# A decoder step whose decode work is moved ahead of stick-breaking and takes six of the sixteen gate chunks, with half of each expert's down projection split

## The reference

```python
u = rmsnorm(x, g_mix); z = u @ w_in        # 1024 -> 3*768 + 3*512 + 2*1024 columns
qa, ka, va, qb, kb, vb, ga, gb = split(z)
oa = combine_groups([dilated(qa[g], ka[g], va[g]) for g in 3 groups])   # 3 x 4 heads
ob = stick_breaking(qb, kb, vb)                                         # 8 heads
x = x + (sigmoid(ga) * (oa @ w_oa) + sigmoid(gb) * (ob @ w_ob)) @ w_out
x = x + hier_moe(rmsnorm(x, g_moe))        # 32 experts, top 2: (silu(v@w_gate) * (v@w_up)) @ w_down
y = rmsnorm(x + sigmoid(rmsnorm(x, g_ple) @ w_pg) * (p @ w_pp), g_final)
```

## Time and profile before

| | us |
|---|---|
| median of 3 runs | 2231.35 (2228.87 to 2236.27) |
| the profiled execution | 2228.89 |
| its span | 2227.3 |
| PE busy in it | 1855.4 (83%) |
| DVE busy | 1057.1 (47%) |
| ACT busy | 800.7 (36%) |
| mean granted clock of TensorE | 0.911 |

### The profile page before, as it was taken

One profiled execution on the slowest core, in us unless ns is written; L12 is line 12 of the kernel. 1 busy time (PEld: TensorE's weight loads), 2 busy tenths in 40 slices (PEclk: granted clock), 3 DMA queues, 4 the chain that ended last, 5 costly groups with the idle time before them and its releaser, 6 DMA issues. The chain is left out here.

```text
span 2227.3 us, 26881 instructions
## 1 busy us (share of the span) xinstructions
PE 1855.4 (83%) x9852; PEld 1443.3 (65%) x9852; DVE 1057.1 (47%) x1415; ACT 800.7 (36%) x1096; POOL 128.4 (6%) x181
## 2 busy tenths in 40 slices
PE   5999999789999947632498992599999999996698
PEld 4999999777777835431295541466666677773585
DVE  5211211158888733335151224466666666662674
ACT  4111111147666503220040000454555555452454
POOL 0111111100000000010031003000000000001110
PEclk7999999989999978675699995699999999998799
DMA  3443444245221160025354213899999999994620
GB/s 114 116 121 114 131 126 122 92 140 172 67 86 39 39 180 1 1 55 152 99 167 145 76 39 137 354 390 379 381 384 385 382 385 382 382 378 164 224 75 39
DMA packets 165325, 401.73 MB, mean 180 GB/s; under 512 B 25659, under 2 KB 102955, under 8 KB 144772
## 3 DMA queue, kind: packets, MB, share of 16 engines
q1 hardware_dynamic: 146004, 334.32, 41.8%
q0 software_dynamic: 10320, 33.82, 5.3%
q10 hardware_dynamic: 8928, 32.63, 3.6%
HBM read 325.80 MB, written 82.61 MB: 183 GB/s over the span
## 5 line engine op out<-in xcount | busy, mean ns | idle before, releaser
L87 PE MATMUL p_acc<-uh,p_wl 128*128 128x344 f32 x720 | 234.9, 326 | 13.0 <-DVE ul L293 9.0
L89 PE MATMUL p_acc<-uh,p_wh 128*128 128x344 f32 x720 | 230.6, 320 | 0.0
L88 PE MATMUL p_acc<-ul,p_wh 128*128 128x344 f32 x720 | 230.5, 320 | 0.0
L1891 PE MATMUL x_Y<-x_wd,x_hT 128*128 128x512 f32 x512 | 225.1, 593 | 0.8 <-DVE x_hT L1989 0.8
L305 DVE COPY p_zk<-p_tp 128x512 f32<-128x512 f32 (+1 forms) x90 | 44.2, 547 | 304.4 <-PE p_tp L226 304.4
L1973 DVE TENSOR_TENSOR x_wgl<-x_wg,x_wgh 128x2048 fp32r<-128x2048 f32 x64 | 143.9, 2290 | 49.8 <-ACT x_wgh L1930 49.8
L1891 PEld LDWEIGHTS x_Y<-x_wd,x_hT 128*128 128x128 f32 x512 | 95.0, 190 | 108.2 <-issue 107.1
L269 ACT ACTIVATE p_zc<-p_acc 128x344 f32<-128x344 f32 x90 | 41.2, 458 | 321.6 <-PE p_acc L89 321.6
L1973 DVE TENSOR_TENSOR x_wul<-x_wu,x_wuh 128x2048 fp32r<-128x2048 f32 x64 | 143.8, 2289 | 17.8 <-ACT x_wuh L1930 17.8
L87 PEld LDWEIGHTS p_acc<-uh,p_wl 128*128 128x128 f32 x720 | 135.8, 189 | 18.0 <-issue 14.9
L545 PE MATMUL g_acc<-uh,g_wl 128*128 128x344 f32 x384 | 129.1, 336 | 9.3 <-ACT u L576 7.1
(11 more groups left out here) (316 smaller groups left out, 3676.8 us busy)
## 6 DMA issues: line engine op xcount, KB each, us to landing
x_wg<-in_w_gate SPq DMA_DIRECT2D x64, 1024.0 KB, 7.7
x_wu<-in_w_up SPq DMA_DIRECT2D x64, 1024.0 KB, 7.4
x_wd<-in_w_down SPq DMA_DIRECT2D x32, 2048.0 KB, 12.5
x_x<-xs SPq DMA_DIRECT2D x32, 512.0 KB, 11.6
ys<-x_y ACTq DMA_DIRECT2D x32, 512.0 KB, 11.8
zT<-p_zc ACTq DMA_DIRECT2D x30, 516.0 KB, 3.4
p_w<-in_w_in SPq DMA_DIRECT2D x30, 512.0 KB, 5.5
ztok<-p_zk POOLq DMA_DIRECT2D x30, 512.0 KB, 4.6
```

The lines of the kernel that those rows point to most:

```text
L87: pe.matmul(out, w_low, m_high, start=first, stop=False)
L88: pe.matmul(out, w_high, m_low, start=False, stop=False)
L89: return pe.matmul(out, w_high, m_high, start=False, stop=last)
L1891: last = pe.matmul(Y[c][:, :], hT[:, k, :], wd[:, b, k, c * 512:(c + 1) * 512], start=(k == 0), stop=(k == KF - 1))
```

## The change

Three edits come together. `decode` becomes `decode_and_gates` and is called ahead of `stick_and_gates`; it takes the first six chunks of gates, and `stick_and_gates` the other ten. In it the attention outputs are computed feature-major at once: the value rows are the stationary operand and the weights of all heads the moving one, so that a product for every pair of heads and features comes out, of which DVE keeps the right ones by a mask and a sum (`own_heads`). The key pages have a buffer of their own (`e_pk`), so that their loads need not wait for K and Q. In `experts`, two of the four k-tiles of `w_down` and of the hidden rows are cut into high and low parts, and `down` uses `products` for them.

```diff
+DECODE_GATES = 6
...
-def stick_and_gates(nc, g):
+def stick_and_gates(nc, g, c0):
...
-        CH = 2 * KD
+        CH = 2 * KD - c0
...
             def load_gate(c):
                 need(sp, gwl_full, c)
-                sp.dma_start(gw[:, :, :], win_v[:, :, QKV + c * P:QKV + (c + 1) * P]).then_inc(gw_in, 16)
+                sp.dma_start(gw[:, :, :], win_v[:, :, QKV + (c0 + c) * P:QKV + (c0 + c + 1) * P]).then_inc(gw_in, 16)
...
-def decode(nc, g):
-
-
...
+def decode_and_gates(nc, g, chunks):
...
-        D_SCORES_T, D_PROBS_T, D_VALUES, D_OUT_T = 3, 4, 5, 7
-        S_SCORES_T, S_WEIGHTS_T, S_VALUES, S_OUT_T = 9, 11, 12, 15
...
+        M = KD * 3
+        GROUPS = chunks * NSPLIT
+        D_SCORES_T, D_PROBS_T, D_VALUES = 6, 7, 8
+        S_SCORES_T, S_WEIGHTS_T, S_VALUES = 13, 14, 16
+        STEPS = GROUPS + 2
+        S_SCORES = {9: (0, 1), 10: (1, 3), 11: (3, 5), 12: (5, 8)}
+        cut_at = {max(0, (c - 1) * NSPLIT): c for c in range(1, chunks)}
...
+            cached(sp, K, 0, 0, kq_in)
+            query(0)
+            sp.wait_ge(cleared, 2)
+            for x in (1, 2):
+                cached(sp, K, 0, x, kq_in)
+                query(x)
+            for x in range(N_DIL):
+                own_row(sp, K, A_W, x, kq_in)
+                own_row(sp, Q, 0, x, kq_in)
...
+            sp.wait_ge(table_in, 16)
+            for b in range(2):
+                for x in range(PG):
+                    load_page(PK, b, x, 0, ek_in[b])
+            cached(sp, V, 1, 0, v_in)
+            sp.wait_ge(cleared, 3)
+            for x in (1, 2):
+                cached(sp, V, 1, x, v_in)
+            for x in range(N_DIL):
+                own_row(sp, V, 2 * A_W, x, v_in)
+            for b in range(2, DEC):
+                for x in range(PG):
+                    load_page(PK, b, x, 0, ek_in[b])
+            sp.wait_ge(scored, 2)
             for b in range(DEC):
-                sp.dma_start(e_bias[b * H_B:(b + 1) * H_B, :], g["b_sb"].rearrange("a (h x) -> (a h) x", x=1))\
-                    .then_inc(ebias_in, 16)
-            sp.wait_ge(table_in, 16)
-            for c in range(CH):
-                if c == D_SCORES_T - 1:
-                    sp.wait_ge(scored, 2)
-                    load_pages(0, ek_in)
-                if c == S_SCORES_T:
-                    sp.wait_ge(es_full, DEC * PG)
-                    load_pages(1, ev_in)
+                for x in range(PG):
+                    load_page(PV, b, x, 1, ev_in)
+            for j in range(2):
+                sp.wait_ge(g_out[j], 16 * ((chunks + 1 - j) // 2))
...
+            def own_heads(dst, src, full, heads):
+                dve.wait_ge(full, 1)
+                n = src.shape[1]
+                m = masked[:, 0:n * DEC * heads].rearrange("p (c b h) -> p c b h", c=n, b=DEC)
+                for c in range(n):
+                    ins = dve.tensor_tensor(m[:, c, :, :], src[:, c, :, :],
+                                            own[:, c, 0:heads].unsqueeze(1).to_broadcast([P, DEC, heads]), ALU.mult)
+                    if c < n - 1:
+                        ins.then_inc(dve_step, 1)
+                        steps[0] += 1
+                    else:
+                        then(ins)
+                dve.tensor_reduce(dst, m, AX, ALU.add).then_inc(done, 1)
+
...
+            cut(0)
+            for n in range(STEPS):
+                if n in cut_at:
+                    cut(cut_at[n])
+                if n == D_SCORES_T - 4:
+                    dilated_scores(0)
+                    dilated_scores(1)
+                if n == D_SCORES_T:
...
+                for b in range(*S_SCORES.get(n, (0, 0))):
+                    stick_scores(b)
...
+            def cut(c):
+                act.wait_ge(gw_in, 16 * (c + 1))
+                need(act, acc_full, (c - 1) * NSPLIT)
+                act.activation(gwh[:, c % 2, :, :], gw[:, :, :], ACT.Copy).then_inc(gwh_full, 1)
+                if c + 1 < chunks:
+                    act.wait_ge(gwl_full, c + 1)
+                    load_gate(c + 1)
...
+            def gates(grp):
+                c, x = divmod(grp, NSPLIT)
+                t = slice(x * NS, (x + 1) * NS)
+                pe.wait_ge(gwl_full, c + 1)
+                need(pe, gate_full, grp - 2)
+                for kk in range(KD):
+                    last = products(pe, acc[grp % 3][:, 0:NS], gwh[:, c % 2, kk, :], gwl[:, c % 2, kk, :], uh[:, kk, t],
+                                    ul[:, kk, t], kk == 0, kk == KD - 1)
+                last.then_inc(acc_full, 1)
...
+            def outputs_T(o, rows_, weights, heads, b0, b1):
+
+                for b in range(b0, b1):
+                    for c in range(o.shape[1]):
+                        for x in range(2):
+                            last = pe.matmul(o[:, c, b, :], rows_(x, b)[:, c * P:(c + 1) * P],
+                                             weights[:, x, b * heads:(b + 1) * heads], start=(x == 0), stop=(x == 1),
+                                             skip_group_check=True)
+                return last
...
+                    outputs_T(oT_ps, lambda x, b: V[:, x, b, :], pT, H_G, 0, DEC).then_inc(oT_full, 1)
...
+                if n in (S_VALUES, S_VALUES + 1):
+                    if n == S_VALUES:
+                        pe.wait_ge(aT_read, 1)
+                        pe.wait_ge(ev_in, 16 * DEC * PG)
+                    b0 = (n - S_VALUES) * DEC // 2
+                    last = outputs_T(eoT_ps, lambda x, b: PV[:, b, x, :], aT, H_B, b0, b0 + DEC // 2)
+                    if n > S_VALUES:
+                        last.then_inc(eoT_full, 1)
+                if n < GROUPS:
+                    gates(n)
...
+        KS = KF // 2
+        wdh, wdl = (sb(n, [P, KS, D], F32R) for n in ("wdh", "wdl"))
+        hh, hl = (sb(n, [P, KS, P], F32R) for n in ("hh", "hl"))
+        hT = sb("hT", [P, KF - KS, P])
...
-                pe.wait_ge(hT_full, n + 1)
+                pe.wait_ge(hl_full, n + 1)
                 pe.wait_ge(d_in[b], it * 16 + 16)
                 need(pe, y_read, n * 2)
                 for k in range(KF):
+                    if k < KS:
+                        pe.wait_ge(dl_full, n * KS + (k + 1))
                     for c in range(2):
-                        last = pe.matmul(Y[c][:, :], hT[:, k, :], wd[:, b, k, c * 512:(c + 1) * 512],
-                                         start=(k == 0), stop=(k == KF - 1))
+                        cols = slice(c * 512, (c + 1) * 512)
+                        if k < KS:
+                            last = products(pe, Y[c][:, :], hh[:, k, :], hl[:, k, :], wdh[:, k, cols], wdl[:, k, cols],
+                                            k == 0, False)
+                        else:
+                            last = pe.matmul(Y[c][:, :], hT[:, k - KS, :], wd[:, b, k, cols], start=False,
+                                             stop=(k == KF - 1))
                 last.then_inc(d_used, 1)
...
+            def high_down(n, b, it):
+                act.wait_ge(d_in[b], it * 16 + 16)
+                need(act, d_used, n)
+                for k in range(KS):
+                    act.activation(wdh[:, k, :], wd[:, b, k, :], ACT.Copy).then_inc(dh_full, 1)
+
+            def high_hidden(n):
+                act.wait_ge(tph_full, n + 1)
+                act.activation(hh[:, :, :], tph[:, 0:KS, :], ACT.Copy).then_inc(hh_full, 1)
...
             def step(it, j):
-                one, three = lag(it, j, 1), lag(it, j, 3)
+                one, two, three = lag(it, j, 1), lag(it, j, 2), lag(it, j, 3)
                 new = it * 2 + j
                 if three:
                     output(*three)
+                if two:
+                    high_down(*two)
                 if one:
                     sigmoid(one[0])
+                if two:
+                    high_hidden(two[0])
                 high(new, wg, wgh, wg_in, g_full, gh_full)
...
                 output(last - 1, 0, np_ - 1)
+                high_down(last, 1, np_ - 1)
+                high_hidden(last)
                 output(last, 1, np_ - 1)
...
-                dve.tensor_copy(hT[:, :, :], tph[:, :, :]).then_inc(hT_full, 1)
+                dve.wait_ge(hh_full, n + 1)
+                dve.tensor_copy(hT[:, :, :], tph[:, KS:KF, :]).then_inc(hT_full, 1)
+                dve.tensor_tensor(hl[:, :, :], tph[:, 0:KS, :], hh[:, :, :], ALU.subtract).then_inc(hl_full, 1)
+
+            def low_down(n, b):
+                for k in range(KS):
+                    dve.wait_ge(dh_full, n * KS + (k + 1))
+                    dve.tensor_tensor(wdl[:, k, :], wd[:, b, k, :], wdh[:, k, :], ALU.subtract).then_inc(dl_full, 1)
...
+                if two:
+                    low_down(two[0], two[1])
...
-            stick_and_gates(nc, g)
+            decode_and_gates(nc, g, DECODE_GATES)
+            stick_and_gates(nc, g, DECODE_GATES)
...
             dilated(nc, g)
-            decode(nc, g)
             clear(nc, range(second, nc.free_semaphores[0]))
```

(6 more changed lines are left out.)

279 lines of the change are left out of this document (119 added, 160 removed).

## The result

| | before | after |
|---|---|---|
| median, us | 2230.11 (4 runs, 2223.57 to 2236.27) | 2203.03 (4 runs, 2197.95 to 2208.75) |
| the profiled execution, its span | 2228.89, 2227.3 | 2207.64, 2206.0 |
| mean granted clock of TensorE | 0.911 | 0.910 |

The ratio is 0.988, 95% interval 0.9837 to 0.9923: faster by 1.2%. The forecast was 2190, with a range of 2164 to 2215: the time came 13 us above it and inside the range, and the gain is 27 us where 41 were forecast.

What follows compares the result with a forecast made beforehand. PE was taken as the bound in stick-breaking (92%, DVE close) and the experts (DMA engines 3% behind). Terms -124 + 134 - 41 - 10 = -41 from 2228.89 gave 2188, 2190 on the median's scale; range 2164 to 2215.

Steps and rivals of the forecast that it cites:

- The case that the forecast described: Whole kernel: the forecast itself, 2190 us with its own range 2177 to 2202, chance 0.50.
- the rival "stretched": New block: one raw gate-weight buffer and late loads make it 156 us, total 2212; chance 0.14.
- Old block -124: Old decode block between `dilated` and `merge`: all its 124 us go.
- New block +134: Decode and six gate chunks ahead of stick-breaking: adds 134 us, bounds 120 to 156.
- K, Q and the gate weights, up to the probabilities at 48: New block's start: loads, cuts and softmax done by 48 us; PE, finished at 41.5, stands 6.5.
- DVE's key products, done at 89.5: New block: two cuts and eight key products of 2.46 us, from 68.5 to 89.5; PE stands 8 us.
- the last part, 94 to 129.5: End of new block: gate groups 14 to 17 take 15.4 us and the stick outputs 20.
- Stick-breaking -41: Stick-breaking with ten gate chunks: DVE becomes the bound, 4.14 us per unit; 41 us saved.
- one of the signs that I had named for being wrong: Stick-breaking: a clock under 1 (forecast 1.00) would show the prediction wrong.
- the slower rival: Stick-breaking: PE granted 1.2 GHz in parts; whole 41 us gain gone at share 0.34, 2280 at 0.6; chance 0.04.
- Experts -10: Experts: 18.7 us per block instead of 19.2, -15 over 30 blocks, +5 at loop end; bounds -16 to +5.
- End of the loop, a stand of some 6 us: Experts' loop end: PE stands some 6 us ahead of the last `down`, costing +5.

Runs made afterwards that it cites:

- two_buffers: Changed kernel with a second raw buffer for the gate weights in the new block, chunk c+2 loaded when chunk c is cut: ratio 0.9809 to before.
- held_back: Changed kernel, single buffer, with SP's loads of V and later pages waiting until gate chunk 2 is cut: ratio 0.9819 to before.
- early_scores: two_buffers with five of the eight stick-breaking key products moved ahead of the cut they were queued behind on DVE: ratio 0.9743 to before.
- full_width: two_buffers with all output products of the new block padded to 64 moving columns: ratio 0.9741 to before.
- five_chunks: two_buffers with five gate chunks ahead instead of six, the sixth back in stick-breaking: ratio 0.9762 to before.
- together_five: two_buffers with early key products, output products 64 columns wide, three cut k-tiles and five gate chunks ahead: ratio 0.9655 to before, median 2154.05 us.
- three_cut: two_buffers with three of the four k-tiles of `down` in the experts cut instead of two: ratio 0.978 to before.
- spread: Changed kernel with the narrow output products placed four behind each k-tile of gate groups 8, 16 and 17, not in batches: ratio 0.99 to before.
- together: two_buffers with early key products, output products 64 columns wide and three cut k-tiles, six chunks ahead: ratio 0.9669 to before, median 2155.75 us.

## Why the prediction was right, and where it was off

The sign came, the time lies 0.6% above the forecast and in the range, and the gain is two thirds of the one forecast. The case that the forecast described did not quite come: its own range ended at 2202, and the new block took 157 us, which is the 156 of the rival "stretched", with the cause that this rival named, one raw buffer and late gate weights (its 156 was added up from other parts, K and Q 10 us later and dearer output products, and these did not come). The time stayed under that rival's 2212 mostly because the experts gained 6 us more than forecast. So part of the closeness is luck: two errors of opposite sign. By its own steps:

- **Old block -124:** came.
- **New block +134, measured 157.** This is the term that was mis-sized, in three places.
  - *K, Q and the gate weights, up to the probabilities at 48: measured 59.9.* The rival "stretched" was set aside by a mean, 164 GB/s over 134 us. But the transfers are asked for at the start: the window of the first 57 us shows 296 GB/s with the engines at full share. For K and Q I had added 4 us for this. DVE's first product came 28.5 us into the block instead of 24, straight behind the cut of chunk 1 and not behind K and Q; in two_buffers, where that cut was early, it waited 3.34 us for them and came at 27.6, so they too were some 4 late, at hardly any cost to PE (a stand of 0.36 us there). For the gate weights I had added nothing and kept the 8 us of the earlier trace rows. held_back shows contention as the cause for chunk 2 (14.0 to 3.9 us); for chunk 1, 15.3 us beside K and Q, the same is likely and not shown. two_buffers shows what late weights cost: 15 us at the probabilities, the forecast's own stand of 6.5 included.
  - *DVE's key products, done at 89.5: measured 105.4,* 4 more than the first place explains. I had put groups 7 and 8 ahead of the dilated outputs; in the list only 7 is, and the cut of chunk 4 waits for group 8, which ran at half clock. early_scores shows, on two buffers, that this queue, and not the pages, made PE stand. The stand itself was forecast, 8 us against 9.01.
  - *Clock.* I had given half clock 2 us at the start, and none later. Group 13 took 6.7 us instead of 4.5 after the stand, and the last part, 94 to 129.5, was forecast at 35.5 and took 41. full_width removes the half clock in and behind the output products, 11.6 us at the mark; group 13 still takes 6.1 there, behind its stand.
- **Stick-breaking -41: -39.3.** 53 scans in 219 us are 4.13 us per unit (4.14 forecast), DVE is busy at 92% (202.07 of 219) as forecast, PE at 86% instead of 82%. The difference is clock, 0.95 instead of 1.00, one of the signs that I had named for being wrong: the mechanism of the slower rival is there, but PE's 3.54 us per unit against the forecast 3.38 are a twentieth of the work at half clock, and not a third. The size came; its reason did so only in part. The forecast made DVE the bound and PE's slack free, yet in five_chunks and together_five one more chunk of PE work made the block 8 and 9.7 us longer, so PE's work still counts there.
- **Experts -10: -16.4.** The limit that I took for the DMA engines was wrong. Multiplying a block's 19.2 us by the share of 97% gave 18.6; it ran at 18.5, PE's full gain, and in three_cut, with 9.3 us less over 31 intervals, at 18.2. The Trainium skill's ceiling in "DMA: Bandwidth & Descriptors", section "Where 436 GB/s comes from", which I cited and did not follow, was nearer: 405 GB/s in three_cut is past the 391 that 379 at 97% stands for.
- **End of the loop, a stand of some 6 us:** 6.37.

## What to carry to other kernels

When independent work is moved beside a stage that begins with loads, look at when each transfer is asked for and not at the mean rate of the stage: a load on which an engine's whole list waits should have a buffer ahead, or be kept clear of transfers that are needed later. Ask of each in-order list what stands behind a wait; here, evictions and key products stood behind cuts. Where products with few moving columns stand among wide ones, compare the price of padding them: it was negative here. And an engine that is not the busiest isn't free for that reason: ask by a run what a piece of work costs on either side.

## What the runs showed of the hardware

- PE, busy without a gap but with matmuls of 8 moving columns among wide ones, was granted 1.2 GHz (spread, 0.50 from 575 to 590). A batch of 64 records with 64 moving columns took 7.25 us (full_width, together), one with 8 took 8.57 to 11.48 (two_buffers, three_cut), because the clock fell in it: at full clock 32 narrow records took 3.63 (early_scores).
- The DMA engines' busy share is no measure of what is left: 0.97 at 379 GB/s (before), 0.99 at 398 (changed kernel), 1.00 at 405 (three_cut) in the same loop, and 1.06 at 296 in the first 57 us of the new block.
- A load of 0.5 MB took 14.0 us from issue to cut beside the loads of V and pages, and 3.9 us without them (held_back, chunk 2).
- One unchanged block, `dilated`, took from 186 to 202 us with a granted clock of 0.81 to 0.71, depending on the kernel (or the execution) around it.
